# Turning the feed-forward products for the down projection by a DMA instead of by TensorE

## The reference

```
def swiglu(x, w_in, w_out):
    gate, up = jnp.split(x @ w_in, 2, axis=-1)
    return (jax.nn.silu(gate) * up) @ w_out

x = x + 0.5 * swiglu(rms_norm(x, ffn1_norm_g[i]), ffn1_w_in[i], ffn1_w_out[i])
...
h = h + swiglu_2(rmsnorm(h, norm_ffn_w[i]), w_gate[i], w_up[i], w_down[i])
```

## Time and profile before

| | |
|---|---|
| median of 3 runs | 1596.38 us (1595.97 to 1598.0) |
| the profiled execution, its own time | 1596.77 us |
| its span, first to last instruction | 1594.8 us |
| PE busy | 1576.4 us, 99% of the span |
| DVE busy | 976.5 us, 61% |
| ACT busy | 816.0 us, 51% |
| GpSimd busy | 71.9 us, 5% |
| DMA | 282.90 MB, mean 177 GB/s |
| granted TensorE clock | 0.999 of full speed |

### The profile page before, as it was taken

How to read it: one execution, slowest core, us unless ns; L and a number is a source line. 1 busy time by engine, 2 the same in 40 slices (tenths; PEclk the granted TensorE clock), 3 DMA queues, 4 the chain that set the end, 5 groups by cost and what they waited for, 6 DMA issues and landing times.

```text
span 1594.8 us, 21992 instructions
## 1 busy us (share of the span) xinstructions
PE 1576.4 (99%) x8615; PEld 1355.8 (85%) x8615; DVE 976.5 (61%) x1118; ACT 816.0 (51%) x993; POOL 71.9 (5%) x76
## 2 busy tenths in 40 slices
PE   8999999999999999999999999999999999999998
PEld 7888888988888888888988888899998899888886
DVE  5664456666544564545687545479998556664444
ACT  6644454465444464445557444466887434464444
POOL 1000000010000000000000000000472000000000
PEclk9999999999999999999999999999999999999999
DMA  7565555445565555555324555556554665555552
GB/s 237 196 208 189 195 169 186 135 147 176 178 207 184 179 190 185 174 195 169 122 80 142 197 190 183 194 176 212 173 173 158 212 188 185 181 186 196 184 189 74
DMA packets 212512, 282.90 MB, mean 177 GB/s; under 512 B 9404, under 2 KB 179800, under 8 KB 212440
## 3 DMA queue, kind: packets, MB, share of 16 engines
q1 hardware_dynamic: 211208, 280.59, 54.0%
q10 hardware_dynamic: 1232, 1.31, 0.2%
HBM read 280.78 MB, written 1.09 MB: 177 GB/s over the span
## 4 chain that ended last, share of the span: by engine, by line
PE 93%; DVE 3%; ACT 2%; issue 1%; POOL 1%; DMA 0%; SPq 0%; POOLq 0%; DVEq 0%; ACTq 0%
PE ps L2057 23%; PE ps L2059 23%; PE ps L2058 23%; PE ps L2049 6%; PE ps L2050 5%; PE ps L2051 5%; PE ps L2224 2%; PE ps L2195 1%; DVE xg_lo L1222 0%; PE ps L2306 0%; DVE w_lo L1192 0%; DMA scr<-in_mem_dram 0%; POOL scr L639 0%; ACT xg_hi L694 0%; PE ps L2570 0%
## 5 line engine op out<-in xcount | busy, mean ns | idle before, releaser
L1192 DVE TENSOR_TENSOR w_lo<-w_raw,w_hi 128x2048 fp32r<-128x2048 f32 x257 | 590.1, 2298 | 286.8 <-ACT w_hi L674 286.6
L674 ACT ACTIVATE w_hi<-w_raw 128x2048 fp32r<-128x2048 f32 x257 | 491.2, 1913 | 387.4 <-PE ps L2059 326.8
L2057 PE MATMUL ps<-w_hi,xg_hi 128*128 128x512 f32 x1008 | 395.1, 392 | 0.6
L2059 PE MATMUL ps<-w_hi,xg_lo 128*128 128x512 f32 x1008 | 392.5, 389 | 0.0
L2058 PE MATMUL ps<-w_lo,xg_hi 128*128 128x512 f32 x1008 | 392.2, 389 | 0.0
L2057 PE MATMUL ps<-w_hi,y_hi 128*128 128x512 f32 (+1 forms) x634 | 253.5, 400 | 0.0
L2059 PE MATMUL ps<-w_hi,y_lo 128*128 128x512 f32 (+1 forms) x634 | 247.3, 390 | 0.0
L2058 PE MATMUL ps<-w_lo,y_hi 128*128 128x512 f32 (+1 forms) x634 | 246.5, 389 | 0.0
L2049 PE MATMUL ps<-xg_hi,w_hi 128*128 128x256 f32 x808 | 231.9, 287 | 1.2 <-DVE xg_lo L1222 0.5
L2050 PE MATMUL ps<-xg_lo,w_hi 128*128 128x256 f32 x808 | 228.5, 283 | 0.0
L2051 PE MATMUL ps<-xg_hi,w_lo 128*128 128x256 f32 x808 | 228.5, 283 | 0.0
(11 more groups left out here) (325 smaller groups left out, 1168.0 us busy)
## 6 DMA issues: line engine op xcount, KB each, us to landing
w_raw<-in_ffn_w_in_dram SPq DMA_DIRECT2D x176, 512.0 KB, 4.6
w_raw<-in_ffn_w_out_dram SPq DMA_DIRECT2D x88, 512.0 KB, 4.2
w_raw<-in_w_in_dram SPq DMA_DIRECT2D x82, 512.0 KB, 4.6
w_raw<-in_a_w_in_dram SPq DMA_DIRECT2D x30, 512.0 KB, 4.4
w_raw<-in_w_gate_dram SPq DMA_DIRECT2D x22, 512.0 KB, 3.7
w_raw<-in_w_up_dram SPq DMA_DIRECT2D x22, 512.0 KB, 4.7
w_raw<-in_w_down_dram SPq DMA_DIRECT2D x22, 512.0 KB, 4.2
w_raw<-in_w_ssd_proj_dram SPq DMA_DIRECT2D x16, 512.0 KB, 4.5
```

Of the source, the lines that this page charges most:

```text
L674: act.activation(w_hi[:, u % RING, :], w_raw[:, u % RING, :], ACT.Copy).then_inc(w_rounded, 1)
L1192: dve.tensor_tensor(w_lo[:, s, :], w_raw[:, s, :], w_hi[:, s, :].bitcast(F32), ALU.subtract).then_inc(w_split, 1)
L2057: pe.matmul(dst, xh, hi, start=start, stop=False, skip_group_check=True)
L2059: return pe.matmul(dst, xl, hi, start=False, stop=stop, skip_group_check=True)
```

## The change

In all chunks of a layer but the last, the hidden products are no longer transposed by PE. The 32-bit floats are handled as pairs of 16-bit halves, since the transposing DMA moves 2-byte elements.

- GpSimd separates the two halves of `h_s` into planes, one copy of 128x512 16-bit elements for each token half (`cut`, waits for `ffn_h`).
- ACT issues one transposing DMA of 128x1024 16-bit elements (256 KB), SBUF to SBUF, at the end of its step (`turn_back`, waits for both cuts).
- GpSimd joins the planes to 32-bit words again, one copy of 128x1024 elements (`join`, waits for the DMA and for DVE to have read the chunk before).
- ACT's `hidden_high` and DVE's `hidden_low` read the joined tile `h_t` in SBUF, not PSUM bank 6, and both stand one step later: behind the first round (split) of the next step.
- The last chunk of each layer is transposed by PE as before.
- PE's `gate_up` waits for `ffn_h` itself before it overwrites banks 4 and 5. ACT's loop is written out, and the last two chunks are taken out of the loops of PE and DVE in every layer.

```diff
+        h_words = KB(16, 2).bitcast(U16).rearrange("p (w b c) -> p w b c", w=2, b=4)
+        h_sent = KB(16, 2).bitcast(U16)
+        h_back = KB(18, 2).bitcast(U16).rearrange("p (b t) -> p b t", t=P)
+        h_t = tiles(KB(20, 2))
...
+            def ffn(f):
+                base = (NI - 1) * nth[f]
+
+                def cut(i):
+                    for tt in range(2):
+                        pool.wait_ge(ffn_h, 2 * (NI * nth[f] + i) + tt + 1)
+                        pool.tensor_copy(h_words[:, :, tt::2], h_s[:, tt].bitcast(U16).rearrange("p (b c w) -> p w b c", w=2, c=P)).then_inc(ffn_cut, 1)
+
+                def join(i):
+                    pool.wait_ge(ffn_back, 16 * (base + i + 1))
+                    pool.tensor_copy(KB(20, 2).bitcast(U16).rearrange("p (b t w) -> p w b t", w=2, t=P),
+                                     h_back.rearrange("p (w b) t -> p w b t", w=2)).then_inc(ffn_joined, 1)
+
+                cut(0)
+                join(0)
+                for i in range(1, NI - 1):
+                    cut(i)
+                    pool.wait_ge(ffn_hl, NI * nth[f] + i)
+                    join(i)
...
+                def turn_back(i):
+                    act.wait_ge(ffn_cut, 2 * ((NI - 1) * nth[f] + i) + 2)
+                    act.dma_start_transpose(out=h_back, in_=h_sent).then_inc(ffn_back, 16)
+
                 def hidden_high(i, p):
-                    act.wait_ge(ffn_ht, NI * nth[f] + i + 1)
-                    act.activation(y_hi[:, 2 * p:2 * p + 2], tiles(ps[:, 6, :]), ACT.Copy).then_inc(ffn_hh, 1)
-
-                def step(g, i, p, it=0, first=False):
+                    act.wait_ge(ffn_joined, (NI - 1) * nth[f] + i + 1)
+                    act.activation(y_hi[:, 2 * p:2 * p + 2], h_t, ACT.Copy).then_inc(ffn_hh, 1)
+
+                def step(g, i, p, it=0, last=False):
                     round_(g + 2, it)
-                    if first:
-                        hidden_high(0, 0)
+                    hidden_high(i - 1, 1 - p)
                     round_(g + 3, it)
                     for tt in range(2):
                         silu(g, i, tt, it)
                     round_(g + 4, it)
-                    hidden_high(i, p)
+                    if last:
...
+                    else:
+                        turn_back(i)
 
                 silu(u, 0, 0)
                 round_(u + 3)
                 silu(u, 0, 1)
-                step(u + 2, 1, 1, first=True)
+                turn_back(0)
+                step(u + 2, 1, 1)
...
                 for i in (1, 2):
-                    gate_up(u + 3 * i - 1, 0, first=2 * NI * nth[f] + 1 if i == 1 else None)
-                    if i == 1:
-                        hidden(0)
+                    gate_up(u + 3 * i - 1, 0, first=taken(i - 1))
                     gate_up(u + 3 * i, 1)
...
-                    down(u + 3 * i + 1, i - 1, (i - 1) % 2, start=i == 1, hidden=lambda: hidden(i))
+                    down(u + 3 * i + 1, i - 1, (i - 1) % 2, start=i == 1)
```

More of the change, by code:

```diff
@@ L20 @@
 I32 = mybir.dt.int32
+U16 = mybir.dt.uint16
 ALU = mybir.AluOpType
@@ L177, in build @@
         ffn_gu, ffn_silu, ffn_h, ffn_ht, ffn_hh, ffn_hl = (sem(n) for n in ("ffn_gu", "ffn_silu", "ffn_h", "ffn_ht", "ffn_hh", "ffn_hl"))
+        ffn_cut, ffn_back, ffn_joined = (sem(n) for n in ("ffn_cut", "ffn_back", "ffn_joined"))
         vec_done, act_done, pe_done, pool_done = (sem(n) for n in ("vec_done", "act_done", "pe_done", "pool_done"))
@@ L656, in ssd @@
                         squares(i)
+            def ffn(f):
[14 more added lines that the diff above has]
+                    join(i)
             for name, _, _ in PHASES[:-1]:
-                if name in ("mixa", "ssd"):
+                if name.startswith("ffn"):
+                    ffn(int(name[3:]))
+                elif name in ("mixa", "ssd"):
                     {"mixa": mixa, "ssd": ssd}[name]()
@@ L769, in step @@
                     round_(g + 4, it)
-                    hidden_high(i, p)
+                    if last:
+                        act.wait_ge(ffn_ht, nth[f] + 1)
+                        act.activation(y_hi[:, 2 * p:2 * p + 2], tiles(ps[:, 6, :]), ACT.Copy).then_inc(ffn_hh, 1)
+                    else:
+                        turn_back(i)
                 silu(u, 0, 0)
@@ L783, in ffn @@
                         act.activation(rope[:, j], rope[:, j], ACT.Sin).then_inc(act_done, act_(f"rope {j}"))
[L784 to L791, removed]
+                for i in range(3, NI):
+                    step(u + 3 * i - 1, i, i % 2, last=i == NI - 1)
             def mem(n, gain):
@@ L1307, in product, with hidden_low, step @@
                                                  op0=ALU.mult, op1=ALU.mult).then_inc(ffn_h, 1)
-                def hidden_low(i, p):
+                def hidden_low(i, p, h=None):
                     dve.wait_ge(ffn_hh, NI * nth[f] + i + 1)
-                    dve.tensor_tensor(y_lo[:, 2 * p:2 * p + 2], tiles(ps[:, 6, :]), y_hi[:, 2 * p:2 * p + 2].bitcast(F32),
+                    dve.tensor_tensor(y_lo[:, 2 * p:2 * p + 2], h_t if h is None else h, y_hi[:, 2 * p:2 * p + 2].bitcast(F32),
                                       ALU.subtract).then_inc(ffn_hl, 1)
                 extra = iter(()) if f > 1 else rope_angles() if f else mem_keys()
-                def step(g, i, p, it=0, more=False, first=False):
+                def step(g, i, p, it=0, more=False, last=False):
                     split(g + 2, it)
-                    if first:
-                        hidden_low(0, 0)
+                    hidden_low(i - 1, 1 - p)
                     if more:
@@ L1326, in step @@
                         next(extra, None)
-                    hidden_low(i, p)
+                    if last:
+                        hidden_low(i, p, tiles(ps[:, 6, :]))
                     split(g + 4, it)
@@ L1333, in ffn @@
                 split(u + 3)
-                step(u + 2, 1, 1, more=f == 1, first=True)
+                step(u + 2, 1, 1, more=f == 1)
                 if f == 0:
@@ L1345, in ffn @@
                 bodies = (NI - 3) // 2
-                peel = f"ffn{f}" == LAST
-                with dve.Fori(0, bodies - peel) as b:
+                with dve.Fori(0, bodies - 1) as b:
                     step(u + 8, 2 * b + 3, 1, b)
                     step(u + 11, 2 * b + 4, 0, b)
-                if peel:
-                    step(u + 8 + 6 * (bodies - 1), NI - 2, 1)
-                    step(u + 11 + 6 * (bodies - 1), NI - 1, 0)
+                step(u + 8 + 6 * (bodies - 1), NI - 2, 1)
+                step(u + 11 + 6 * (bodies - 1), NI - 1, 0, last=True)
             def mem(n, gain, factor):
@@ L2229, in down, with taken @@
                     d_unit(v, it, y0=2 * p, **kw)
+                def taken(i):
+                    return 2 * (NI * nth[f] + i) + 1
                 for i in (1, 2):
[L2232 to L2234 removed]
+                    gate_up(u + 3 * i - 1, 0, first=taken(i - 1))
                     gate_up(u + 3 * i, 1)
@@ L2238, in ffn @@
                         pe.wait_ge(vec_done, vec.at("M ksum"))
-                    down(u + 3 * i + 1, i - 1, (i - 1) % 2, start=i == 1, hidden=lambda: hidden(i))
-                with pe.Fori(0, (NI - 3) // 2) as b:
+                    down(u + 3 * i + 1, i - 1, (i - 1) % 2, start=i == 1)
+                bodies = (NI - 3) // 2
+                with pe.Fori(0, bodies - 1) as b:
                     for j in range(2):
-                        gate_up(u + 8 + 3 * j, 0, b)
+                        gate_up(u + 8 + 3 * j, 0, b, first=taken(2 * b + 2 + j))
                         gate_up(u + 9 + 3 * j, 1, b)
-                        down(u + 10 + 3 * j, 2 * b + 2 + j, j, b, hidden=lambda: hidden(2 * b + 3 + j))
+                        down(u + 10 + 3 * j, 2 * b + 2 + j, j, b)
+                v = u + 6 * (bodies - 1)
+                for j in range(2):
+                    gate_up(v + 8 + 3 * j, 0, first=taken(NI - 3 + j))
+                    gate_up(v + 9 + 3 * j, 1)
+                    down(v + 10 + 3 * j, NI - 3 + j, j, hidden=(lambda: hidden(NI - 1)) if j else None)
                 down(u + 3 * NI - 1, NI - 1, 0, norm=n + 1)
```

## The result

| | before | after |
|---|---|---|
| median | 1596.47 us (4 runs, 1595.97 to 1598.0) | 1609.86 us (4 runs, 1607.3 to 1614.53) |
| the profiled execution, its own time | 1596.77 us | 1614.53 us |
| its span | 1594.8 us | 1612.8 us |

The changed kernel is slower: the ratio of the times is 1.0086, with a 95% interval from 1.0061 to 1.011. Its profiled execution is the slowest of its four, 4.7 us above their median; what follows explains that execution, with its 18.0 us of added span.

What follows compares the result with a forecast made beforehand. PE, busy for 99% of the span, was taken as the bound. 1596.77 - 23.0 for removed transposes + 8.2 for first-chunk stalls = 1582.0, less 0.4 for the median 1581.6, predicted as 1582 us; range 1575 to 1660.

Steps and rivals of the forecast that it cites:

- rival A: Slower: the turn of the hidden products bounds every chunk, from L = 8.6 on; 1660 us at L = 9.8; chance 0.24.
- What the change removes: PE's 50 sets of four transposes in five layers, 0.46 us each, 23.0 us, all on the path.
- The copies: On GpSimd, 0.62 us per cut and 1.24 per join; up to 2.3 us more for a copy during a split.
- L: Time from ACT's issue of the transposing DMA to its landing, taken as 5.3 us, bounds 2.5 and 9.8.
- Steady chunks: Chunks after each layer's first: 45 of the 50 turns are hidden behind PE, with 3.8 us to spare.
- A's ring: From one `y_hi` to the next: 6.5 us to DMA issue, 7.75 + L in all, passing PE's 16.32 from L = 8.6.
- First chunks: Before each layer's first down unit PE stalls L - 3.65, 1.65 us, in five layers 8.2 us.
- Rival B: No difference: with L between 7.6 and 8.7 the first chunks eat the gain, 1594 to 1600 us; chance 0.08.
- Rival C: Slower: DMA engines full if the transpose moves 64-byte pieces, 9.8 us per chunk, near 2060 us; chance 0.04.

Runs made afterwards that it cites:

- e2: Changed kernel, but DVE starts the split behind the products only when both cuts are done; 1573.16 us, ratio to before 0.9851.
- e5: Changed kernel with chunk 0 of each layer turned by PE again and DVE waiting for both cuts before the third split; 1575.54 us, ratio to before 0.9868.
- e7: Changed kernel with chunk 0 turned by PE, DVE waiting for cuts before the third split, and GpSimd's first join per layer repeated six times as delay; 1602.22 us.
- e3: Changed kernel with a plain DMA of the same bytes for the transposing one, values wrong, only timing counts; 1585.41 us, one run.

## Why the prediction was wrong

The forecast was faster, 1582 us; the kernel is slower, 1609.86, inside the range but by the mechanism of rival A, which had 0.24.

- **What the change removes: right.** 23.0 us forecast. e2, where nothing waits, has a span 22.9 us below that of before (1594.8 less 1571.9) and the forecast chunk of 16.32.
- **The copies: right.** A cut takes 0.61 and a join 1.34 us where nothing holds them (0.62 and 1.24 forecast), a held cut 2.61 (2.52 for the operation in the earlier trace rows).
- **L as one number: the first half of the error.** I took 5.3 from loads beside others, and every later step used that one value. In the changed kernel its median is 3.6 where the last weight load went out 2 to 2.5 us earlier, and it is 5.9 to 9.4, median about 7, behind a load issued under 0.5 us earlier. The mean of the two would have been a fair guess, but few chunks see the mean. Over the 375 transposing DMAs of the eight runs that have them the median falls in order: 7.0 us at under 0.5 us behind a load, 5.1 at 0.9 to 1.3, 4.2 at 1.5 to 2.0, 3.6 at 2.0 to 2.5, 3.1 at over 3. So most of L hangs on when it is issued, which the change itself decides. Not all of it: 9.51 came 0.97 us behind a load, and 7.36 (in e5) 2.08 us behind one.
- **Steady chunks "hidden, with 3.8 us to spare", and A's ring of "7.75 + L" closing at L = 8.6: the step that failed.** I followed one chunk that starts on time, and there it holds: in the layer 2 chunk above, whose down unit starts at 480.76, `y_hi` begins 7.5 us later (488.27), where I had 11.1. For the late chunk I wrote "two products 0.96, a cut 0.62, about 6.5 us with hand-overs" from `y_hi` to the DMA's issue. Measured: 8.48 (965.34 to 973.82). The 2.0 us are the hold of a cut by a split, which I knew and priced at 2.3, and used for chunk 0 alone. A late `y_hi` makes ACT and DVE run back to back, so the split follows the products at once, in every late chunk. Without the hold the ring is 7.9 + L (e7's turn from 603.41 to 616.28, 12.87 us with a landing of 4.96), near my 7.75; with it 9.97 + L, and it closes at L = 6.35, not 8.6. The same lateness pushes L above that. The two terms were in my text, but as independent of each other and of the state the chunk is in.
- **First chunks: formula right, size off.** L - 3.65 with the measured L of 6.21 gives 2.56 us; PE waited 2.46. The five sum to 11.7, not 8.2. What I didn't ask is what such a gap leads to: the forecast let it end with its chunk.
- **Rival A: right kind, wrong condition.** Its signs came (a period above 16.5 with gaps ahead of down units), in three layers of five, at a median L of 7.2 in the late turns where it asked for 8.6. Its 1660 was too much, since the ring passes 16.32 by about 1 us.
- **Rival B** fits the size of the first step only: by the measured gaps alone the sum would be 1596.8 - 23.0 + 11.7 = 1585.5, near e3's 1585.41.
- **Rival C: wrong.** The DMA moves 1056 packets per turn ((54032 - 1232) / 50) of 248 bytes, each 24 ns (0.049 x 16 x 1612.8 / 52800), and the weight loads land after 4.6 us as before.
- **The Trainium skill.** VectorE: DVE Perf Modes, section "The three transpose paths", by whose 1309 ns per block I estimated an L of 10.5: no landing reached it (9.5 at most), and the usual one is 3.7; the measurement decides against adding blocks up. Advanced Engine Details and Errata, section "X-Bar Transpose (TRN2)", that transposing DMAs are as fast as plain ones: agrees where no load is fresh (medians 3.7 against 3.6) and nearly where one has just gone out whole (6.0 to 6.2 against 5.5 to 6.2), not between the halves of a load (9.4 and 7.7 against 5.7 and 4.5), and not at the issue (1.25 against 0.47 us of ACT's queue).

## What to carry to other kernels

Where work goes round a ring of engines beside the bottleneck, cost the ring twice: for a turn that starts on time and for one that starts late, since a late turn packs instructions together that a timely one keeps apart, and its locks and transfers get longer. If the late ring is longer than the bottleneck's period, one late turn can keep all later ones late, as in layers 3 to 5 here, and the slack of the timely ring says nothing about it. The cure can be a wait: a split with microseconds of slack that lets a 0.6 us copy go first gained 2.3% on the changed kernel (1609.86 to 1573.16), and 1.5% on the one before.

## What the runs showed of the hardware

**The clock behind a gap.** PE's gap ahead of layer 2's first down unit was 2.46 us; the unit then took 7.20 us, not 5.44. The window behind it with PE alone (us, PE busy, granted clock, DMA share, GB/s):

```profile
397.40:401.00 3.60, 3.60 (x10) 0.60 0.23 94
```

In e7, behind a gap of 4.48 us (all engines; the clock is the third value from the end):

```profile
604.80:609.00 4.20, 4.18 (x10) 3.31 (x11) 3.08 (x3) 3.57 (x4) 0.38 (x1) 0.50 0.00 0
```

A granted clock of 0.50 is the lower level, 1.2 GHz; the matmuls at that level stand 0.43 us apart at either place, not 0.2264 (the 0.60 is the mean of a stretch that is at the lower level for most of its time). So this gap cost 4.5 us of waiting and 3.0 us of slower matmuls (8.47 less 5.44), and a gap of 2.46 cost 1.76 more. It isn't a matter of length alone: layer 1's first gap, 2.46 us as well, was followed by a down unit of 5.52, and layer 3's, 2.23 us, by one of 5.57. In the changed kernel the lower level shows inside a layer only in layer 2 behind this gap and in layer 3 behind the second one (2.78 us, then a down unit of 7.00). In layer 2 it is nearly all of the loss after the gap (18.08 in place of 16.32); in layer 1, with much the same distance of 18.07, it has no part: there PE waited a second time, for 1.50 us.

**The spread.** The changed kernel's four runs lie 7.2 us apart, e2's 2.3. A pace held by landing times of 6 to 9 us would pass their scatter on to the total, and a pace set by PE would not; that is my reading, no run tests it.
